# Branch gates of a streaming encoder layer: seven half-size products for a pair of units in place of plain products

## The reference, cut to what matters

```
h @ w_in  ->  q_lat, c_kv, k_r, f_q, f_k, f_v, f_logit, m_q, g       # g: 3 x 1024 columns
gates = sigmoid(g).reshape(b, s, 3, 1024)
attention A (latent), B (forgetting), C (256 memory tokens) -> o_mla, o_fox, o_mem
y  = gates[0] * (o_mla @ w_br_mla) + gates[1] * (o_fox @ w_br_fox) + gates[2] * (o_mem @ w_br_mem)
x1 = LayerNorm(ALPHA * h + y @ w_out)
out = LayerNorm(ALPHA * x1 + MoE(x1))        # 64 experts, top 8, and one shared expert
```

## Time and profile before

| | |
|---|---|
| median of 3 runs | 1135.76 us (1135.4 to 1136.64) |
| the profiled execution, its own time | 1135.26 us |
| its span | 1133.5 us |
| PE busy | 1104.6 us, 97% |
| DVE busy | 449.1 us, 40% |
| ACT busy | 208.8 us, 18% |

### The profile page before, as it was taken

The page is one execution under the profiler, slowest core; times in us unless marked ns, Lnnn a source line. Parts: engine busy times, 40 slices in busy tenths (PEclk is TensorE's granted clock), DMA queues, the critical chain, the costliest instruction groups (busy, mean ns, idle before and its releaser), DMA issues.

```text
span 1133.5 us, 16219 instructions
## 1 busy us (share of the span) xinstructions
PE 1104.6 (97%) x6074; PEld 618.5 (55%) x6074; DVE 449.1 (40%) x1163; ACT 208.8 (18%) x389; POOL 77.3 (7%) x84
## 2 busy tenths in 40 slices
PE   8999999999999999999999999999999999999994
PEld 3455546666666655457555555555555554554551
DVE  0141014445444333256574434424424434434426
ACT  1222116654334200001011011011011011011012
POOL 2100000000000000001014400000000000000000
PEclk9999999999999999999999999999999999999998
DMA  9532265223655588743489999999999999999981
GB/s 325 189 103 74 80 219 181 70 85 127 237 196 182 177 289 336 306 128 108 173 353 371 392 396 401 408 379 385 403 388 392 405 394 391 408 387 389 397 340 58
DMA packets 82886, 312.29 MB, mean 276 GB/s; under 512 B 13032, under 2 KB 26128, under 8 KB 56584
## 3 DMA queue, kind: packets, MB, share of 16 engines
q1 hardware_dynamic: 65136, 278.08, 62.8%
q0 software_dynamic: 6560, 15.65, 4.5%
q10 hardware_dynamic: 11136, 17.83, 4.5%
HBM read 305.46 MB, written 10.95 MB: 279 GB/s over the span
## 4 chain that ended last, share of the span: by engine, by line
PE 95%; DVE 3%; DMA 1%; issue 1%; ACT 0%; SPq 0%; ACTq 0%; DVEq 0%
PE ps_P L1247 20%; PE ps_P L990 11%; PE ps_V L1272 10%; PE ps_V L1261 10%; PE ps_P L898 7%; PE ps_V L1183 5%; PE ps_S L1261 5%; PE ps_P L906 4%; PE ps_V L1192 4%; PE ps_T L1236 3%; PE ps_T L889 2%; PE ps_V L1224 1%; PE ps_P L1031 1%; DMA xT<-x_t 1%; PE ps_S L1254 1%; PE ps_V L957 1%
## 5 line engine op out<-in xcount | busy, mean ns | idle before, releaser
L1247 PE MATMUL ps_P<-arena,branch_out 128*64 128x256 f32 (+1 forms) x2176 | 233.6, 379 | 0.7 <-DVE branch_out L1880 0.7
L1247 PEld LDWEIGHTS ps_P<-arena,branch_out 128*64 128x64 f32 (+1 forms) x2176 | 152.0, 135 | 90.3 <-issue 19.3
L990 PE MATMUL ps_P<-xT,weight_ring 128*128 128x384 f32 x384 | 136.8, 491 | 0.0
L1901 DVE TENSOR_TENSOR branch_out<-branch_out,ps_P 128x256 f32<-128x256 f32 x33 | 13.9, 421 | 286.0 <-PE ps_P L1247 286.0
L1261 PE MATMUL ps_V<-weight_ring,branch_out 128*128 128x512 f32 x264 | 124.1, 592 | 0.0
L1442 ACT ACTIVATE weight_ring<-ps_V,merge 128x512 f32<-128x512 f32 x66 | 45.3, 687 | 414.0 <-PE ps_V L1272 414.0
L1272 PE MATMUL ps_V<-arena,branch_out 128*64 128x512 f32 (+1 forms) x544 | 120.6, 598 | 0.0
L1924 DVE TENSOR_TENSOR x_sb<-x_sb,ps_V 128x512 f32<-128x512 f32 x132 | 90.7, 687 | 17.4 <-PE ps_V L1261 17.4
L990 PEld LDWEIGHTS ps_P<-xT,weight_ring 128*128 128x128 f32 x384 | 68.9, 190 | 37.9 <-issue 2.5
L1272 PEld LDWEIGHTS ps_V<-arena,branch_out 128*64 128x64 f32 (+1 forms) x544 | 34.8, 135 | 77.2 <-issue 60.4
L1261 PEld LDWEIGHTS ps_V<-weight_ring,branch_out 128*128 128x128 f32 x264 | 47.9, 191 | 47.3 <-issue 47.3
(11 more groups left out here) (326 smaller groups left out, 1054.2 us busy)
## 6 DMA issues: line engine op xcount, KB each, us to landing
arena<-w_e_gate SPq DMA_DIRECT2D x68, 1024.0 KB, 8.6
arena<-w_e_up SPq DMA_DIRECT2D x68, 1024.0 KB, 10.5
arena<-w_e_down SPq DMA_DIRECT2D x68, 1024.0 KB, 7.3
weight_ring<-w_in SPq DMA_DIRECT2D x12, 1024.0 KB, 9.2
weight_ring<-w_in ACTq DMA_DIRECT2D x8, 1024.0 KB, 6.7
gates<-arena ACTq DMA_DIRECT2D x24, 192.0 KB, 3.9
arena<-fox_k_t SPq DMA_DIRECT2D x8, 512.0 KB, 4.1
arena<-cache_fox_v SPq DMA_DIRECT2D x8, 512.0 KB, 4.8
```

Source lines behind the costliest of these rows:

```text
L990: last = mm(out[:, 0:T], slot[:, k % 4, m * P:(m + 1) * P], xT[:, k, :], start=(k == 0), stop=(k == KD - 1))
L1247: last = mm(bank[r:r + wide, 0:256], xgT[q][:, k, r:r + wide], w[h][:, k, :], start=(k == 0), stop=(k == KD - 1))
```

## The change

Two neighbouring gate units (256 gate channels) are computed together. Their weights form a 2x2 block matrix: A11, A21 are the first four input blocks of the first and second unit, A12, A22 the last four. The input is cut into X11, X12 (first four blocks, tokens 0 to 191 and 192 to 383) and X21, X22 (last four blocks). Eight half products become seven, with sums of weights and inputs in front and sums of the results behind. `x_dif` = X12 - X11, `x_all` = X22 - x_dif, `x_end` = X22 - X12, `x_low` = X21 - x_all; `w_sum` = A21 + A22, `w_less` = w_sum - A11, A21 is overwritten by A11 - A21 and A12 by A12 - w_less.

Each product is a piece: four matmuls of 128 x 128 weights and 192 columns. There are 12 pairs, so 84 pieces. The order of the list changes as well: ("norm", n - 1) stands in front of the gate pieces, the first piece of a slot in front of the transposes, the others behind the values, and a new stage ("weights", i, m), one DVE sum each, behind the first piece of the slot:

```diff
+    s.append(("inputs",))
+    s += [("weights", 0, m) for m in range(3)]
     s += [("T", "mk", j) for j in range(2)]
...
+    pieces = [("W", i, r) for i in range(TWO) for r in range(7)]
+    n_pieces = len(pieces)
     def gate_piece():
+        st = pieces.pop(0)
+        s.append(st)
+        i, r = st[1:]
+        if r == 3:
+            mixes.append(("weights", i, 3))
+        elif r >= 4 and i + 1 < TWO:
+            mixes.append(("weights", i + 1, r - 4))
...
         if 1 <= n <= n_u:
             s.append(("norm", n - 1))
+        due = 0
+        while (len(pieces) - due) * (n_u + 4) > n_pieces * (n_u + 3 - n):
+            due += 1
+        if due:
+            gate_piece()
+        s += mixes
+        mixes.clear()
         if 2 <= n <= n_u + 1:
             s.append(("T", "p", n - 2))
         if 3 <= n <= n_u + 2 and values_at(U, n - 3) == n - 3:
             s.append(("V", "o", n - 3))
+        for _ in range(due - 1):
+            gate_piece()
```

On PE a piece r of pair i waits for the sums it reads and for its bank (the two banks of ring P in turn):

```diff
+            def gate_product(i, r):
+                w, x = ((a11, xT[:, 0:4, 0:HALF]), (w_less, x_all), (a12, xT[:, 4:KD, 0:HALF]), (a21, x_end),
+                        (w_sum, x_dif), (a22, x_low), (a12, xT[:, 4:KD, HALF:T]))[r]
...
+                elif r == 3:
+                    pe.wait_ge(w_mixed, 4 * i + 3)
+                    pe.wait_ge(w_read, 7 * i + 1)
+                elif r == 4:
+                    pe.wait_ge(w_read, 7 * i + 2)
...
+                for k in range(4):
+                    last = mm(gate_bank(i, r), w[:, k, :], x[:, k, :], start=(k == 0), stop=(k == 3))
+                last.then_inc(done["W"], 1)
```

On DVE the sums of weights are 128x512 in SBUF, those of the inputs 128x768 (once), and every result but the first is added from PSUM into a buffer of the pair, 128x192 each, two adds for r = 4:

```diff
+                elif ring == "weights":
+                    if m == 0:
+                        if i:
+                            dve.wait_ge(done["W"], done_at("W", i - 1, 4))
+                        for n in (0, 1):
+                            at = first_of["g"] + i // 2 * 2 + n
+                            dve.wait_ge(w_loaded[at % NW], loads_of(at))
+                        V.tensor_tensor(w_sum, a21, a22, ALU.add).then_inc(w_mixed, 1)
...
+                    elif r == 3:
+                        dve.wait_ge(w_read, 7 * i + 1)
+                        V.tensor_tensor(c21, out, c12, ALU.add).then_inc(w_read, 1)
+                    elif r == 4:
+                        dve.wait_ge(w_read, 7 * i + 3)
+                        V.tensor_tensor(c22, out, c21, ALU.add).then_inc(w_read, 1)
+                        V.tensor_tensor(c12, out, c12, ALU.add).then_inc(w_read, 1)
```

ACT copies the first result of a pair (128x192), and one sigmoid of 128x768 in SBUF serves a pair, at the second piece of the next pair; stores and reloads of gates follow, 12 stores of 384 KB in place of 24 of 192 KB. Chunks are loaded behind the seventh piece of every second pair:

```diff
+            def make_gates(i):
+                act.wait_ge(w_read, 7 * i + 7)
+                fn(gate_two[i % 2], gate_two[i % 2], ACT.Sigmoid).then_inc(gate_made, 1)
...
+                    if r == 0:
+                        if i >= 2:
+                            act.wait_ge(gates_stored, 16 * (i - 1))
...
+                        fn(gate_two[i % 2][:, 0, 0:HALF], gate_bank(i, r), ACT.Copy).then_inc(w_copied, 1)
+                    elif r == 1 and i:
+                        make_gates(i - 1)
+                    elif r == 6 and i % 2 and i // 2 + 2 < 6:
+                        w_load(act, first_of["g"] + i + 3)
+                        w_load(act, first_of["g"] + i + 4)
```

The new buffers (`gate_two`, `x_mix`, `w_sum`, `w_less`) take the place in `arena` where the caches of the running streams lay, and the caches move onto the attention buffers of the new stream (`kcat`, `qcat`, `fqA`, `fkA`). So SP gets a wait before the first cache load, and the stores of the forgetting keys count on a semaphore of their own, which SP, POOL and the DVE stage "inputs" wait for:

```diff
             for b in range(NB):
                 if b >= 2:
                     wait_unit("mla", b - 2, "V")
+                if b == 0:
+                    sp.wait_ge(done["V"], done_at("V", "o", 4 * H // 2 - 1))
```

More of the change, by code:

```diff
@@ L219, in plan @@
     s.append(("V", "c", "p"))
[L221 removed]
+    pieces = [("W", i, r) for i in range(TWO) for r in range(7)]
+    n_pieces = len(pieces)
     def gate_piece():
[L224 to L225 removed]
+        st = pieces.pop(0)
[5 more added lines that the diff above has]
+            mixes.append(("weights", i + 1, r - 4))
+    mixes = []
     n_u = len(U)
@@ L369, in build @@
         w_kv = A.take(1024)
+        prompt_at = A.at
+        kcat = A.take(H, 256)
+        qcat = A.take(H, 256)
+        v_mla = A.take(2, 512)
+        fqA = A.take(H, 256)
+        fkA = A.take(H, 256)
         late = A.at
+        lat_all = A.take(1280)
+        lat_raw = lat_all[:, 0:TT * 424].rearrange("p (j c) -> p j c", j=TT)
         w_q = A.take(2, 768)
-        lat_raw = A.take(TT, 424)
         fk_tok = A.take(TT, 512)
@@ L376, in build @@
         qnT = A.take(2, T)
-        mk_tok = lat_raw.rearrange("p j c -> p (j c)")[:, 0:1024].rearrange("p (j c) -> p j c", j=2)
-        fqA = A.take(H, 256)
-        fkA = A.take(H, 256)
+        mk_tok = lat_all[:, 0:1024].rearrange("p (j c) -> p j c", j=2)
         assert A.at <= a_cols - T
+        Z = Space(R_A, a_cols, late)
+        gate_two = [None, Z.take(2, T)]
+        Z.take(512)
+        x_mix = [Z.take(4, HALF) for _ in range(4)]
+        gate_two[0] = Z.take(2, T)
+        w_sum, w_less = Z.take(4, P), Z.take(4, P)
         OE = Space(R_O, o_cols)
@@ L390, in build @@
         gkv_b = YE.take(128)
[L392 to L397, removed]
+        B = Space(R_A, a_cols, prompt_at)
+        fkTc, mkTc, fvc, mvc = ([] for _ in range(4))
+        for i in range(2):
+            fkTc.append(B.take(4, 256))
+            mkTc.append(B.take(4, 256))
+            fvc.append(B.take(2, 512))
+            mvc.append(B.take(2, 512))
+            B.take(1024)
         L = Space(lngb, lngb_cols)
@@ L491, in build @@
         ps = {r: [ctx.enter_context(nc.psum_tensor(f"ps_{r}{i}", [P, 512], F32)) for i in range(2)] for r in "PSTV"}
-        done = {r: sem(f"{r}_done") for r in "PSTV"}
+        done = {r: sem(f"{r}_done") for r in "PSTVW"}
         free = {r: sem(f"{r}_free") for r in "PSTV"}
@@ L622, in ln2_shift, with gate_weights, gate_bank, loads_of @@
             return eng.scalar_tensor_tensor(x_sb[:, j, :], scaled[j], rst[:, j:j + 1], lngb[:, D:2 * D], ALU.mult, ALU.add)
+        def gate_weights(i):
+            n, m = first_of["g"] + i // 2 * 2, i % 2 * 2
+            s0, s1 = wring[:, n % NW], wring[:, (n + 1) % NW]
+            a, b = slice(m * P, (m + 1) * P), slice((m + 1) * P, (m + 2) * P)
+            return s0[:, :, a], s1[:, :, a], s0[:, :, b], s1[:, :, b]
+        def gate_bank(i, r):
+            return ps["P"][(7 * i + r) % 2][:, 0:HALF]
+        def loads_of(n):
+            return sum(0 if WU[m][0] == "lat" else 16 for m in range(n + 1) if m % NW == n % NW)
         block = ctx.enter_context(nc.Block())
@@ L881, in w_wait @@
             def w_wait(n):
[L883 to L886, removed]
+                pe.wait_ge(w_loaded[n % NW], loads_of(n))
+                return wring[:, n % NW]
             def tr(out, in_, n):
@@ L981, in values @@
                 last.then_inc(done["V"], 1)
[L983 to L992, removed]
+            def gate_product(i, r):
+                a11, a12, a21, a22 = gate_weights(i)
+                x_dif, x_all, x_end, x_low = x_mix
+                w, x = ((a11, xT[:, 0:4, 0:HALF]), (w_less, x_all), (a12, xT[:, 4:KD, 0:HALF]), (a21, x_end),
+                        (w_sum, x_dif), (a22, x_low), (a12, xT[:, 4:KD, HALF:T]))[r]
+                if r == 0:
+                    w_wait(first_of["g"] + i // 2 * 2)
+                    if i:
+                        pe.wait_ge(w_read, 7 * i - 1)
+                    else:
+                        pe.wait_ge(free["P"], done_at("P", "mv", 1))
+                elif r == 1:
+                    pe.wait_ge(x_mixed, 4)
+                    pe.wait_ge(w_mixed, 4 * i + 2)
+                    if i:
+                        pe.wait_ge(w_read, 7 * i)
+                elif r == 2:
+                    w_wait(first_of["g"] + i // 2 * 2 + 1)
+                    pe.wait_ge(w_copied, i + 1)
+                elif r == 3:
[3 more added lines that the diff above has]
+                    pe.wait_ge(w_read, 7 * i + 2)
+                elif r == 5:
+                    pe.wait_ge(w_read, 7 * i + 3)
+                else:
+                    pe.wait_ge(w_mixed, 4 * i + 4)
+                    pe.wait_ge(w_read, 7 * i + 5)
+                for k in range(4):
+                    last = mm(gate_bank(i, r), w[:, k, :], x[:, k, :], start=(k == 0), stop=(k == 3))
+                last.then_inc(done["W"], 1)
             def slot_tokens(n, par):
@@ L1386, in _ @@
                     last.then_inc(free["P"], 1)
[L1387 to L1392, removed]
+                elif ring == "W":
+                    i, r = key
+                    if r == 0:
+                        if i >= 2:
+                            act.wait_ge(gates_stored, 16 * (i - 1))
+                        if i == 1:
+                            act.wait_ge(done["T"], done_at("T", "mk", 1))
+                            act.wait_ge(stored, 16 * PROJ_STORES)
+                        act.wait_ge(done["W"], done_at(*st))
+                        fn(gate_two[i % 2][:, 0, 0:HALF], gate_bank(i, r), ACT.Copy).then_inc(w_copied, 1)
[4 more added lines that the diff above has]
+                        w_load(act, first_of["g"] + i + 4)
                 elif ring == "V" and key[0] == "b":
@@ L1396, in _ @@
```

(6 more changed lines are left out.)

112 lines of the change are left out of this document (79 added, 33 removed).

## The result

| | before | after |
|---|---|---|
| median of the runs | 1135.74 us (1135.4 to 1136.64) | 1124.3 us (1122.41 to 1124.67) |
| profiled execution: own time, span | 1135.26, 1133.5 | 1122.41, 1120.6 |

The ratio is 0.9893, 95% interval 0.9881 to 0.9906: 1.07% faster. Forecast were 1124.9 in a range of 1119 to 1132.

What follows compares the result with a forecast made beforehand. PE, busy 97% of the span and practically all the attention, was taken as the bound. 1135.26 - 12.9 saved on PE + 2.0 of stalls = 1124.4 us profiled, median 1124.9; range 1119 to 1132 for 8 in 10.

Steps and rivals of the forecast that it cites:

- PE's term: Gate matmuls on PE: 672 records of 192 columns at 0.165 us replace 123.8 us, saving 12.9 us (8.2 to 15.6).
- the places between: Attention slots with gate pieces in front of and behind the values: extra transitions cost nothing, 0 to 16 x 0.1 us.
- DVE's term: Adds and sums put on DVE: 63.3 us more; first attention part busy 90.9 of about 104 us, 87%.
- The stalls that I set at 2.0 us: PE waiting for late DVE in the attention's first part: 0.25 us in each of 7 pairs, 0.2 at the end.
- The slack of 0.8 us: Transposed copy in an attention slot: DVE ends it about 3.4 us after the slot began, PE asks at 4.2.
- The order of normalisation: Attention slots: normalisation now in front of the gate piece; behind it the scores would have almost no slack; no size given.
- ACT and DMA at nothing: ACT loses some 25 us of work, cost 0 (6 without cover); DMA waits cost 0, up to 2 if late.
- the likeliest case: Whole execution with stalls of 0 to 5 us: 1119.5 to 1128 us, chance 0.66.
- Rival 4: Expert stretch: if DMA sets its end, the time gained is given back and 1135 us remained; chance 0.05.
- DVE as the pace of the first part: First attention part: each of 29 pieces with a sum costs 0.2 to 0.4 us, say 1131 us; chance 0.17.
- The round trip: Transposed copy behind add and sum: PE stands until DVE works off each slot, 32 us less 12.9, 1155; chance 0.08.
- Records that don't shrink: Gate matmuls: weight load of 0.190 us sets the distance, 127.7 us, 1141 with stalls; chance 0.04, including unhidden loads.

Runs made afterwards that it cites:

- plain_192: The kernel before with each gate matmul cut into two of 192 columns, without the seven products: 1136.79 us, ratio 1.0006.
- second_in_front: The changed kernel with the second gate piece of the 16 two-piece slots put directly behind the first: 1123.83 us, ratio 0.9896 against the kernel before.
- extra_1: The changed kernel with one more unused DVE operation behind each weight sum from the second pair on: 1131.48 us, ratio 0.9967 against the kernel before.
- norm_behind: The changed kernel with normalisation put back behind the first gate piece and weight sum of its slot: 1128.72 us, ratio 0.9939 against the kernel before.
- after_again: The changed kernel run once more with no edit: 1122.28 us, ratio 0.9883 against the kernel before.
- all_undone: The changed kernel with normalisation behind the gate pieces, both pieces in front and three sums in one go: 1134.32 us, ratio 0.9982 against the kernel before.
- extra_2: The changed kernel with two more unused DVE operations behind each weight sum from the second pair on: 1152.58 us, ratio 1.0151 against the kernel before.

## Why the prediction was right, and where its steps were off

**PE's term: right, somewhat small.** I took 0.165 us for a record of 192 columns; it measured 0.1625 within a piece. I had 12.9 us for the saving; plain_192 and the changed kernel give 14.1 to 14.2. The taken value was above the true one because the rows of 128 and 256 columns carried their first record's surplus, as I had seen and only half corrected: behind the first record these start 0.112 and 0.216 apart in the trace of the kernel before, and the middle of the two is 0.164. The rule that I set against it (the Trainium skill, "TensorE: Matmul & The Clock Gate", Part 3: loads overlap only with another row group) would have made the attention longer by some 60 us, by the estimate that the prediction worked out from that page. Both 192-column kernels exclude it, with a record every 0.1625 us and a load record of 0.190 for each.

**No cost at the places between: right.** The 16 slots with a piece behind the values cost nothing measurable, second_in_front differs by 0.4 us.

**DVE's term: the load was mis-sized.** 90.9 us for the first part measured 79.56, and 87% measured 77%, since I summed the lengths of records that overlap by 0.08 to 0.09 us. In the whole span DVE's busy time grew by 50.7 us (449.1 to 499.8), where I had named 63. The stalls that I set at 2.0 us were 0.2: only the one at the end came, as predicted, before L1260. A lighter load than reckoned fits that, but no run separates it from a larger slack.

The slack of 0.8 us at the transposed copy was somewhat high. The terms that the prediction lists in front of the copy (0.45, 1.3, 0.2, 0.6, 0.69, 0.42) add up to 3.66 us and not to 3.4. The 3.4 holds for a slot with one add, and with two adds 0.5 us of slack is left. The extra operations measure it. In the first part they stand behind 26 sums, and each puts off what follows by 0.72 us (190.84 to 191.56 in extra_1, from its start to the copy's). One costs 0.27 us per sum there (6.9 / 26), two cost 1.02 (26.4 / 26), of which up to 0.23 is a slower clock (last section). What was absorbed is the difference, 0.45 and some 0.65 us. That is an estimate of the slack, with DVE catching up in the slots between.

**The order of normalisation: right in mechanism, 6.2 us.** The prediction said that behind the piece there was almost no slack, and norm_behind lost 6.2 us of attention with PE waiting at the scores.

**ACT and DMA at nothing: right.** ACT's busy time fell from 105.0 to 76.2 us in the attention. The first chunk reached DVE at 159.5 and the three sums were over at 161.5, against 162.9 when the copy behind them had its input: a cover of 1.4 us, thinner than the 2.8 that I had reckoned:

```profile
159.47 0.69 DVE L1860 TENSOR_TENSOR arena<-weight_ring 128x512 f32<-128x512 f32 x1 [20.88 <-DMA weight_ring<-w_in]
160.80 0.69 DVE L1866 TENSOR_TENSOR weight_ring<-weight_ring 128x512 f32<-128x512 f32 x1
162.88 1.29 DVE L1771 COPY arena<-ps_T 128x512 f32<-128x512 f32 x2 [1.39 <-PE ps_T L943]
```

**The sum: the mechanism right, the closeness of 0.6 us partly luck.** 10.9 us were forecast for the profiled execution. The attention gave 14.1, since both terms erred to the same side: PE saved more and the stalls stayed out. The expert stretch took 1.1 back (1133.5 - 550.31 = 583.2 before, from the first step's start, 584.28 after), of which the long step has 0.8 and the last work behind the steps 0.3 (PE's wait for ACT's queue there is 2.1 us in place of 1.8). With 0.1 lost on either side of the attention that makes 12.9, 2.0 more than forecast. Between the medians it is only 11.4, because the profiled execution of the changed kernel was the fastest of the four, 1.9 below their median, where I had added 0.5. In after_again median and profiled execution agree (1122.28, 1122.2) and the gain is 13.3. The span that I gave for the likeliest case, 1119.5 to 1128, does not follow from its own terms: 15.6 or 8.2 us saved and 0 to 5 us of stalls give 1120.2 to 1132.6.

The expert stretch was costed at nothing. Rival 4, that all is given back, is out: the steps before the long one last 17.54 or 17.59 us and those behind it 17.54 or 16.97 in both kernels, save the last with 17.07. For the 0.8 us of that one step no cause is shown. Its length varies in either kernel, but DMA is at 0.93 to 0.95 there, so a part of DMA in it is not excluded.

**The rivals.** DVE as the pace of the first part (0.17) did not occur, but is near: it comes at about 85% busy, one operation of 0.69 us more per sum. The round trip (0.08) did not occur either; the extra operations show its place and its price. One such operation costs 0.16 us per sum of the whole attention (7.1 / 44) and leaves a gain, two cost 0.71 (31.3 / 44) and turn it into a loss, with the turning point that I gave, 0.27, between them. Records that don't shrink (0.04) are excluded.

## What to carry to other kernels

Where one engine is busy without a gap, count what a rewriting takes off it in record distances and not in record lengths, and ask of the engine that takes over the work whether each of its results is still in time. The share of busy time does not answer that. In the first part DVE was busy 77% and cost nothing, and with the same work in another order it was at 72% (norm_behind) or 69% (all_undone) and cost 5.7 or 10.5 us. The cheap operation that frees a buffer for the bound engine belongs in front of the new work. To learn how much room is left, put in more of the new work once: here that told more than my reckoning.

## What the runs showed of the hardware

In extra_2 PE stood idle for 3.56 us, and the clock granted to it was at half, 1.2 GHz, for about the next 7 us, though it worked again. Stretches of 2 us, columns as in the earlier trace rows, clock in the last but two:

```profile
194.00:196.00 2.00, 0.00 (x0) 0.00 (x0) 1.93 (x4) 0.00 (x0) 0.00 (x0) 0.99 0.00 0
196.00:198.00 2.00, 1.56 (x9) 1.23 (x10) 1.97 (x7) 0.57 (x2) 0.00 (x0) 0.50 0.12 11
198.00:200.00 2.00, 2.00 (x7) 1.82 (x6) 1.93 (x5) 0.00 (x0) 0.00 (x0) 0.50 0.90 274
200.00:202.00 2.00, 2.00 (x8) 1.91 (x8) 0.91 (x5) 0.90 (x3) 0.00 (x0) 0.50 1.05 407
202.00:204.00 2.00, 2.00 (x12) 1.81 (x13) 0.98 (x4) 1.71 (x3) 0.00 (x0) 0.81 0.95 354
```

So a stall that DVE causes is paid a second time on PE: a piece of 8 records there (198.51 to 201.07) takes 2.56 us and not 1.30. The same came once more, from 254.0 to about 257.4, behind a wait of 2.81 us that ended at 253.1. Up to 6 us of extra_2's 31 are this, an estimate from PE's busy time in the first part, 111.17 us against 105.18 in extra_1 for the same products. In extra_1 the longest wait was 2.1 us, and its clock stayed at 1.00 in both parts.

The prediction read the clock as at its upper level in all slices of the kernel before. The last digit of that row is 8, before and after the change: PE has no work in about the last 10 us.
